# Second attention of a two-block transformer: value products with the values as stationary operand, two heads side by side, results already turned

## The chip, the cores and the metric

One Trainium2 chip, one of its cores. The metric is the device time of one execution in microseconds (us). TensorE is written PE in the profile, VectorE DVE, ScalarE ACT, GpSimd POOL, SyncE SP.

## The reference

Two transformer blocks on 512 tokens of width 1024, all in float32. The first has differential and stick-breaking attention and a convolved feed-forward network (FFN). The second has an FFN, a hybrid mixer and another FFN. The change lies in the mixer's attention and its output projection:

```python
q_a, kv_a, gate_a, q_b, kv_b = jnp.split(proj, offsets, axis=-1)
# heads of 64; 8 "NSA" query heads over 2 key/value heads, 8 "SWA" query heads over 2
o_cmp = jnp.einsum('bgrtc,bcgd->btgrd', p_cmp, vc)               # compressed keys, 31 of them
o_slc = selected_attention(q, ks, vs, sel_idx, slopes)           # top 16 of 8 blocks: all of them
o_win = banded_attention(q, kw, vw, slopes, NSA_WINDOW)          # window 512: the whole causal part
o_a = g[..., 0:1] * o_cmp + g[..., 1:2] * o_slc + g[..., 2:3] * o_win
o_b = banded_attention(q_b, k_b, v_b, slopes, SWA_WINDOW, sinks) # window 128, with a sink
o = jnp.concatenate([o_a, o_b], axis=-1)
return o @ w_out                                                 # 1024 x 1024
```

## The kernel before

All engines run programs written out by hand and joined by semaphores. Weights come from HBM in 1024-column units of 128 partitions through a ring of six slots (`stage`). ACT rounds each unit to `w_hi` (L619), POOL makes the remainder `w_lo` in two halves (L645), and each product is made of three matmuls, hi*hi, hi*lo, lo*hi.

The second attention (`at2`) is a list of 96 items. Items 0 to 63 (groups p = 0 to 3) are NSA heads: for each p and each block i of 128 queries, two branches times two heads g = 0, 1, each with b = i + 1 key blocks of 128. Items 64 to 95 (p = 4 to 7) are SWA heads, two for each i, with b = 1, 2, 2, 2. Items 2k and 2k+1 are always the two heads of a pair. There are 80 key blocks per head side in the NSA pairs together (32 pairs) and 28 in the SWA pairs (16 pairs).

Every engine runs the same loop of steps n, each engine its part of items n, n-1, n-2, ...:

- PE, even n: logits of items n and n+1 (L977): the heads' 64 channels stand on the upper and the lower 64 rows of the array. Every n: a few matmuls of filling, then the turns of item n-2's weights `W` by transposes (L1012), more filling, then the value product of item n-3 (L1019): stationary is the turned weight block (128x128), moving are 64 columns of values, in float32, so each matmul is two records in the trace.
- DVE: takes item n-4's result out of PSUM with the factor 1/sum times gate (L1081, L1078), then item n's logits plus bias with their row minimum (L1110), then for item n-1 reciprocal and gate factor (L1131, L1132, L1135).
- ACT: exp of item n-1 with its sum (L1056, L1057), copy of item n-2's turned weights to SBUF (L1064).

"Filling" is dense work that PE draws from a generator: 9 projection chunks of 24 matmuls and 96 matmuls of the compression's small network (L1262 to L1266), then, from step 84, the output projection: `pe_turn1` turns the finished outputs O (L1163), ACT and DVE split them into `T_hi` (L1187) and `T_lo` (L1200), and `pe_wo1` (L1210) multiplies. The table `FILL2` says how many at each step, with `(early, late)` for before and after the turns, and halves where it has one number:

```python
FILL2 = [4] * 48 + [6] * 4 + [0] + [6] * 4 + [0] + [3] * 8 + [0] + [3] * 8 + [0] + [3] * 8
FILL2 = FILL2 + [(0, 4), 0] + [(0, 4), (3, 0)] * 5 + [(3, 12), (12, 6), 6]
```

The compressed branch is hung on steps 49 to 77 by hooks: its own value product (L1612, four hooks at steps 70 to 76) and `dve_cmp_add` (L1620) add to O. Waits in the turns: `pe.wait_ge(a.exp_done, it.exps)`, that is, ACT's exp alone; DVE's factors come after. After step 99 `pe_wo_rest` makes the rest of the output projection (192 matmuls in all), and the last FFN follows (L548).

Of the kernel before, what the change touches and what calls it, by code (L numbers as in the profile page):

```python
# [39 lines left out]
P = 128  # L40
T = 512
# [65 lines left out]
SPARED = 4  # L107
WO_NEXT = {1: (1,), 3: (2,), 4: (3,), 5: (4,), 6: (5, 6)}
# [4 lines left out]
def unit_order():  # L113
# [11 lines left out]
    return order + [U_WO2 + j for j in WO_ORDER] + list(range(U_UP3, N_UNITS))  # L125
# [29 lines left out]
TURN_ORDER = [[c if kind == "diff" else 4 + c for kind, c in GROUPS1], [0, 1, 2, 3, 4, 6, 5, 7]]  # L155
# [3 lines left out]
FILL2 = FILL2 + [(0, 4), 0] + [(0, 4), (3, 0)] * 5 + [(3, 12), (12, 6), 6]  # L159
# [46 lines left out]
def build(nc, weights, x_t, params, rows, table_t, bias_line, out_t):  # L206
    with ExitStack() as top:
# [98 lines left out]

        def cmp_PT(h):
            return scratch[:, bass.ts(h, P)]
# [117 lines left out]
        n_ffn2 = Norm("ffn2", 7, "fold", X, order=WO_ORDER)  # L426
# [186 lines left out]

        def act_hi(act, u):

            if u < N_UNITS:
                slot = u % RING
                act.wait_ge(loaded[slot], 16 * (u // RING + 1))
                act.activation(w_hi[:, slot, :], stage[:, slot, :], ACT.Copy).then_inc(hi_done, 1)  # L619
# [201 lines left out]

        def item(items, **what):
            items.append(Item(**what))
# [24 lines left out]
        for p in range(8):  # L848
            c, q = p % 4, queries2(p)
            groups2.append(len(items2))  # L850
            for i in range(TB):
                if p < 4:
                    k0, nk, s0 = full(i)
                    for branch in range(2):
                        k = HOME2[("ks", "kw")[branch]]
                        for g in range(2):
# [5 lines left out]
                                 out=O[:, i, bass.ts(h, HD)], add=(branch == 1),  # L862
                                 gate=gates[:, i, 3 * h + 1 + branch:3 * h + 2 + branch], sink=None)
                else:
                    k0, nk = max(i - 1, 0) * P, min(i + 1, 2) * P
                    k = HOME2["kb"]
                    for g in range(2):
# [5 lines left out]
                             out=O[:, i, T + h * HD:T + (h + 1) * HD], add=False, gate=None,  # L873
                             sink=row[:, ROW_SINK + h:ROW_SINK + h + 1])
        for items in (items1, items2):
            pre, at = 0, 0
            for n, it in enumerate(items):
# [4 lines left out]
                it.dv = it.out.shape[-1]  # L882
# [71 lines left out]
        def item_bank(it):  # L954

            return ITEM_PS + it.n % 3

        def pe_attn(pe, a, fill=None, per_item=()):
# [31 lines left out]
            for n in range(len(items) + 3):  # L990
                f = per_item[n] if n < len(per_item) else 0
                early, late = f if isinstance(f, tuple) else (f - f // 2, f // 2)
# [10 lines left out]
                if 2 <= n < len(items) + 2:  # L1003
# [3 lines left out]
                    else:  # L1007
                        pe.wait_ge(a.comb if it.kind == "diff" else a.exp_done, it.exps)
                    if it.n >= 3:
# [5 lines left out]
                if n >= 3:  # L1015
# [9 lines left out]
        def act_attn(act, a, link, after):  # L1025
            items = a.items
            for n in range(len(items) + 2):
# [31 lines left out]
                if n >= 2:  # L1059
                    it = items[n - 2]  # L1060
                    act.wait_ge(a.turned, it.n + 1)
                    if it.n >= 2:
                        act.wait_ge(a.pv_done, it.n - 1)
                    act.activation(WT[:, it.n % 2, 0:it.nk], PS[:, item_bank(it), 0:it.nk],  # L1064
                                   ACT.Exp if it.kind == "sb" else ACT.Copy).then_inc(a.wt_ready, 1)
# [3 lines left out]
        def dve_attn(dve, a, link, after):  # L1069
            items = a.items  # L1070
            for n in range(len(items) + 4):
                if n >= 4:
# [3 lines left out]
                    if it.kind == "soft" and it.add:  # L1076
                        dve.wait_ge(a.o_done, it.n)
                        dve.scalar_tensor_tensor(out=it.out, in0=pv, scalar=it.st[:, 6:7], in1=it.out,  # L1078
                                                 op0=ALU.mult, op1=ALU.add).then_inc(a.o_done, 1)
                    elif it.kind != "sb":  # L1080
# [5 lines left out]
                if n < len(items):  # L1086
# [5 lines left out]
                    if n >= 4:  # L1092
# [21 lines left out]
                if 1 <= n < len(items) + 1 and items[n - 1].kind != "sb":  # L1114
# [14 lines left out]
                    else:  # L1129
# [13 lines left out]
        o_turned = [sem("o_turned1"), sem("o_turned2")]  # L1143
# [4 lines left out]
        def pe_turn1(pe, b, g):  # L1148
            k, bank = TURN_ORDER[b][g], 7
            if b == 0:  # L1150
                pe.wait_ge(o_ready, g + 1)
            elif g < 4:
                pe.wait_ge(cm["used"], TB)
            else:
                pe.wait_ge(at2.o_done, groups2[6] if g < 6 else len(items2))
            if b == 0 and 1 <= g <= SPARED:
# [1004 lines left out]
```

## Time and profile before

| | us |
|---|---|
| median of 3 runs | 1645.12 |
| lowest, highest | 1644.98, 1645.23 |
| profiled execution, span first to last instruction | 1643.2 |
| PE busy | 1623.6 (99%) |
| second attention, first logits to first FFN matmul | 1037.7 to 1271.5 |
| granted TensorE clock | 0.999 of full |

The profiled execution shows 1643.2 us as its span; the timed runs are about 1.9 us longer. Busy PE time includes a matmul's modelled end, so two records that overlap count once and a short pause between matmuls may show as busy.

### The profile page before, as it was taken

The numbers are of one execution on the slowest core, as the hardware profiler recorded it, in microseconds if no ns is written. First come the engines' busy times: TensorE is split into PE (matmuls) and PEld (weight loads), VectorE is DVE, ScalarE is ACT, GpSimd is POOL, SyncE is SP. The second block draws the span as 40 slices with busy tenths as digits, with TensorE's granted clock in tenths as the row PEclk, the third lists the DMA queues.
The fourth block names the chain that finished last, engine by engine and source line by source line (L and its number), as shares of the span: only waits on it lengthen the run. The fifth ranks groups of instructions, "written<-read, shape, count | busy, mean of one in ns | idle before, by whom it ended". The sixth has DMA issues, their size and how long they took to land.

```text
span 1643.2 us, 21043 instructions
## 1 busy us (share of the span) xinstructions
PE 1623.6 (99%) x8100; PEld 1349.0 (82%) x8100; DVE 701.2 (43%) x1404; ACT 674.6 (41%) x1183; POOL 759.2 (46%) x581
## 2 busy tenths in 40 slices
PE   9999999999999999999999999999999999999997
PEld 7787888888888888888888888888888888888886
DVE  7276747874444227322113225555773311112224
ACT  6356645543334325422223224567563422223322
POOL 7424454564445552744445552543114544444550
PEclk9999999999999999999999999999999999999999
DMA  5411102323222231323232322212002222223221
GB/s 205 148 52 52 52 1 103 129 90 103 92 101 95 97 101 61 116 96 102 90 103 90 103 92 101 91 66 78 27 27 96 97 94 99 99 94 103 90 103 51
DMA packets 42115, 147.35 MB, mean 90 GB/s; under 512 B 4768, under 2 KB 5152, under 8 KB 42016
## 3 DMA queue, kind: packets, MB, share of 16 engines
q1 hardware_dynamic: 40680, 143.39, 25.7%
q10 hardware_dynamic: 1336, 2.63, 0.5%
q8 instruction: 64, 1.05, 0.3%
q14 instruction: 35, 0.29, 0.1%
HBM read 142.84 MB, written 3.41 MB: 89 GB/s over the span
## 4 chain that ended last, share of the span: by engine, by line
PE 82%; DVE 2%; issue 1%; ACT 1%; POOL 1%; DMA 0%; DVEq 0%; ACTq 0%; POOLq 0%
PE PS L587 20%; PE PS L589 20%; PE PS L588 20%; PE PS L1210 5%; PE PS L548 4%; PE PS L1221 3%; PE PS L1019 2%; PE PS L556 2%; PE PS L977 2%; PE PS L1012 1%; POOL w_lo L645 0%; DVE L L1110 0%; DMA stage<-in_weights 0%; PE PS L609 0%; ACT sq L1057 0%
## 5 line engine op out<-in xcount | busy, mean ns | idle before, releaser
L645 POOL TENSOR_TENSOR w_lo<-stage,w_hi 128x512 fp32r<-128x512 f32 x522 | 707.9, 1380 | 819.2 <-ACT w_hi L619 818.3
L619 ACT ACTIVATE w_hi<-stage 128x1024 fp32r<-128x1024 f32 x262 | 274.8, 1056 | 519.9 <-DMA stage<-in_weights 516.0
L587 PE MATMUL PS<-H_hi,w_hi 128*128 128x512 f32 x992 | 386.1, 389 | 0.4 <-DVE rcol L1407 0.4
L588 PE MATMUL PS<-H_lo,w_hi 128*128 128x512 f32 x992 | 386.0, 389 | 0.0
L589 PE MATMUL PS<-H_hi,w_lo 128*128 128x512 f32 x992 | 385.9, 389 | 0.0
L587 PEld LDWEIGHTS PS<-H_hi,w_hi 128*128 128x128 f32 x992 | 186.2, 188 | 39.0 <-DVE rcol L1407 0.7
L589 PEld LDWEIGHTS PS<-H_hi,w_lo 128*128 128x128 f32 x992 | 186.2, 188 | 38.9
L588 PEld LDWEIGHTS PS<-H_lo,w_hi 128*128 128x128 f32 x992 | 186.2, 188 | 38.7
L587 PE MATMUL PS<-A_hi,w_hi 128*128 128x512 f32 x528 | 205.6, 389 | 0.3 <-DVE A_lo L756 0.3
L589 PE MATMUL PS<-A_hi,w_lo 128*128 128x512 f32 x528 | 205.4, 389 | 0.0
L588 PE MATMUL PS<-A_lo,w_hi 128*128 128x512 f32 x528 | 205.4, 389 | 0.0
L771 DVE TENSOR_TENSOR conv<-PS,rstd 128x512 f32<-128x512 f32 x88 | 56.5, 686 | 342.8 <-PE PS L589 333.7
L756 DVE TENSOR_TENSOR A_lo<-A,A_hi 128x512 fp32r<-128x512 f32 x66 | 84.0, 1278 | 227.2 <-ACT A_hi L700 227.2
L587 PEld LDWEIGHTS PS<-A_hi,w_hi 128*128 128x128 f32 x528 | 99.1, 188 | 21.7 <-DVE A_lo L756 1.2
L588 PEld LDWEIGHTS PS<-A_lo,w_hi 128*128 128x128 f32 x528 | 99.1, 188 | 20.7
L589 PEld LDWEIGHTS PS<-A_hi,w_lo 128*128 128x128 f32 x528 | 99.1, 188 | 20.4
L1019 PEld LDWEIGHTS PS<-V,tmp 128*128 128x128 f32 x672 | 93.8, 191 | 7.7
L1064 ACT ACTIVATE tmp<-PS 128x256 f32<-128x256 f32 (+3 forms) x144 | 59.4, 412 | 90.4 <-PE PS L1012 89.8
L1019 PE MATMUL PS<-V,tmp 128*128 128x64 f32 (+1 forms) x672 | 91.5, 264 | 0.0
L781 DVE SCALAR_TENSOR_TENSOR conv<-tmp,par,conv 128x511 f32<-128x511 f32 (+1 forms) x88 | 78.2, 944 | 4.3 <-ACT conv L723 4.2
L1221 PE MATMUL PS<-H_hi,w_hi 128*128 128x512 f32 x168 | 74.6, 444 | 0.9 <-DVE QB L940 0.9
L1221 PE MATMUL PS<-H_hi,w_lo 128*128 128x512 f32 x168 | 71.2, 424 | 0.0
(234 smaller groups left out, 2048.2 us busy)
## 6 DMA issues: line engine op xcount, KB each, us to landing
stage<-in_weights SPq DMA_DIRECT2D x262, 512.0 KB, 3.2
out_t<-Y SPq DMA_DIRECT2D x8, 256.0 KB, 2.0
X<-in_x_t SPq DMA_DIRECT2D x3, 512.0 KB, 8.8
bias_line<-bias_line ACTq DMA_DIRECT2D x1, 1270.0 KB
strip<-bias_line ACTq DMA_DIRECT2D x1, 1024.0 KB, 5.0
stage<-in_weights SPq DMA_DIRECT2D x2, 256.0 KB, 4.6
V<-QF SPq DMA_DIRECT2D x4, 128.0 KB, 2.3
V<-QF SPq DMA_DIRECT2D x4, 127.8 KB, 2.4
```

The lines of the kernel that those rows point to most:

```text
L548: pe.matmul(PS[:, j, :], w[:, (u0 + j) % RING, bass.ts(c, P)], H_hi[:, c, :], start=(k == 0 and w is w_hi), stop=False)
L587: pe.matmul(out, a, h_hi, start=first, stop=False, skip_group_check=skip)
L588: pe.matmul(out, a, h_lo, start=False, stop=False, skip_group_check=skip)
L589: return pe.matmul(out, b, h_hi, start=False, stop=last, skip_group_check=skip)
L619: act.activation(w_hi[:, slot, :], stage[:, slot, :], ACT.Copy).then_inc(hi_done, 1)
L645: lo = pool.tensor_tensor(w_lo[:, slot, cols], stage[:, slot, cols], w_hi[:, slot, cols].bitcast(F32), ALU.subtract)
L756: dve.tensor_tensor(A_lo[:, f % DEEP, :], A[:, f, :], A_hi[:, f % DEEP, :].bitcast(F32), ALU.subtract).then_inc(a_lo_done, 1)
L781: dve.scalar_tensor_tensor(out=y, in0=z[j][:, 0:T - back], scalar=c, in1=y, op0=ALU.mult, op1=ALU.add).then_inc(conv_step, 1)
L1019: mm = pe.matmul(PS[:, item_bank(it), 0:it.dv], WT[:, it.n % 2, bass.ts(kb, P)], it.v[kb], start=(kb == 0), stop=(kb == it.nk // P - 1))
L1064: act.activation(WT[:, it.n % 2, 0:it.nk], PS[:, item_bank(it), 0:it.nk], ACT.Exp if it.kind == "sb" else ACT.Copy).then_inc(a.wt_ready, 1)
L1210: mm = pe.matmul(PS[:, j, :], w[:, u % RING, cols], h, start=(g == 0 and x == 0), stop=(g == 7 and x == 2))
L1221: mm = pe.matmul(PS[:, bank, :], w[:, u % RING, bass.ts(k, P)], h[:, k, :], start=(k == 0 and x == 0), stop=(k == KC - 1 and x == 2))
```

## The change

The second attention's value product is turned round. Stationary are 64 columns of values (128 keys), moving the turned weights of 128 queries, and the result lands as 64 channels x 128 queries: head g = 0 on PSUM partitions 0 to 63 and g = 1 on 64 to 127 of bank 5, one call `soft_heads` for a pair, at odd steps, five steps behind its first item. Both branches of a pair accumulate in PSUM. So the 1/sum and gate factors can no longer be put on the result's rows; DVE puts them on the weights `W` (128 x 128b) before the turns, and the turns wait for that (`a.comb`). Outputs no longer need turning: for p < 4 DVE copies a finished 128x128 block to `O_flat`, where the compressed branch's product (also in turned form, 32 matmuls of 64 columns instead of 8) is added, and `act_sum_hi`/`dve_sum_lo` split the sum; for p >= 4 ACT and DVE split straight from PSUM. Weight rows of the output projection have another order, so its 8 units are loaded by four DMAs each. A step's filling stands in one piece behind the turns.

```diff
+WO_ORDER2 = [6, 7, 0, 1, 2, 3, 4, 5]
-    return order + [U_WO2 + j for j in WO_ORDER] + list(range(U_UP3, N_UNITS))
+    return order + [U_WO2 + j for j in WO_ORDER2] + list(range(U_UP3, N_UNITS))
-FILL2 = FILL2 + [(0, 4), 0] + [(0, 4), (3, 0)] * 5 + [(3, 12), (12, 6), 6]
+FILL2 = FILL2 + [0, 0] + [4, 3] * 5 + [1] + [6, 6, 6]
 # items
-out=O[:, i, bass.ts(h, HD)]
+out=PS[g * HD:(g + 1) * HD, HEADS_PS, bass.ts(i, P)]      # HEADS_PS = 5
 # PE
+            def soft_heads(n):
+                it = items[n]
+                if not it.add and n > 0:
+                    pe.wait_ge(a.o_done, 4 * it.group + it.i)
+                pe.wait_ge(a.wt_ready, n + 2)
+                blocks = it.nk // P
+                for kb in range(blocks):
+                    for x in (it, items[n + 1]):
+                        mm = pe.matmul(x.out, x.v[kb], turned_weights(x)[:, bass.ts(kb, P)],
+                                       start=(kb == 0 and not x.add),
+                                       stop=(kb == blocks - 1 and (x.add or x.gate is None)))
+                mm.then_inc(a.pv_done, 1)
-                early, late = f if isinstance(f, tuple) else (f - f // 2, f // 2)
+                early, late = f if isinstance(f, tuple) else (0, f) if a is at2 else (f - f // 2, f // 2)
-                        pe.wait_ge(a.comb if it.kind == "diff" else a.exp_done, it.exps)
+                        pe.wait_ge(a.comb, it.exps)
+                if a is at2:
+                    if n >= 5 and n % 2 == 1:
+                        soft_heads(n - 5)
 # DVE, item n-1
-                        if it.gate is not None:
-                            c = link(dve.tensor_scalar(it.st[:, 6:7], it.st[:, 6:7], it.gate, None, ALU.mult))
-                            after(c)
-                        dve.sem_inc(a.comb, 1)
+                        w = W[:, it.n % 2, 0:it.nk]
+                        if it.gate is None:
+                            dve.tensor_scalar(w, w, it.st[:, 6:7], None, ALU.mult).then_inc(a.comb, 1)
+                        else:
+                            dve.tensor_scalar(w, w, it.st[:, 6:7], it.gate, ALU.mult, ALU.mult).then_inc(a.comb, 1)
 # the splits that replace pe_turn1, act_turn1 and dve_turn1 of the second attention
+        def act_heads_hi(p, i, pair):
+                act.wait_ge(at2.pv_done, pair + 1)
+                act.activation(T_hi[:, p, bass.ts(i, P)], PS[:, HEADS_PS, bass.ts(i, P)], ACT.Copy).then_inc(heads_hi, 1)
+        def dve_heads_lo(p, i):
+                dve.tensor_tensor(T_lo[:, p, cols], PS[:, HEADS_PS, cols], T_hi[:, p, cols].bitcast(F32), ALU.subtract)
 # compressed branch
-                    mm = pe.matmul(PS[:, 7, bass.ts(h % 2, 256)], cmp_PT(h), vc4[:, bass.ts(h // 4, 256)], start=True, stop=True)
+                for i in range(TB):
+                    for g in range(2):
+                        mm = pe.matmul(PS[g * HD:(g + 1) * HD, 7, bass.ts(i, P)], vc4[:, bass.ts(4 * g + i, HD)],
+                                       cmp_PT(4 * g + pair), start=True, stop=True)
 # hooks
+            hook(at2, "act", at + 29 + pair, act_sum_hi(pair))      # steps 78 to 81
+            hook(at2, "dve", at + 30 + pair, dve_sum_lo(pair))      # steps 79 to 82
+        for p in range(8):
+            for i in range(TB):
+                last = groups2[p] + (4 * i + 2 if p < 4 else 2 * i)
+                if p < 4:
+                    hook(at2, "dve", last + 6, dve_heads_out(p, i, last // 2))
+                else:
+                    hook(at2, "act0", last + 6, act_heads_hi(p, i, last // 2))
+                    hook(at2, "dve", last + 6, dve_heads_lo(p, i))
 # loads of the output projection
+                for g in range(2):
+                    for l in range(2):
+                        sp.dma_start(there[bass.ts(g, HD), :, :, l, :],
+                                     here[bass.ts(l, HD), :, g, :, :]).then_inc(loaded[u % RING], 16)
```

## Rows read from the trace of the kernel before

**Rows 1.** Windows: NSA steps, SWA steps, rest of the projection; busy us (x records) of PE, PEld, DVE, ACT, POOL.

```profile
1037.70:1170.70 133.00, 131.91 (x1009) 113.57 (x1008) 78.17 (x341) 86.39 (x226) 48.60 (x36) 1.00 0.21 69
1170.70:1228.40 57.70, 55.59 (x415) 47.01 (x414) 44.24 (x184) 39.24 (x139) 7.56 (x6) 1.00 0.09 29
1228.40:1271.50 43.10, 43.10 (x201) 35.59 (x201) 13.57 (x25) 14.33 (x21) 16.89 (x13) 1.00 0.24 86
```

**Rows 2.** Timeline of PE (start, us, what): a value product, then logits.

```profile
1102.76 1.00 PE L1019 MATMUL PS<-V,tmp 128*128 128x64 f32 x8
1103.69 0.49 PE L977 MATMUL PS<-K_f,QF 64*128 64x128 f32 x4
```

**Rows 3.** Timeline of PE: logits and turns; column-tiled products; the small network's filling.

```profile
1224.19 0.71 PE L977 MATMUL PS<-B_f,QB 64*128 64x128 f32 x8
1224.84 0.44 PE L1012 MATMUL PS<-ident,sq 128*128 128x128 f32 x2
...
1141.05 0.43 PE L1019 MATMUL PS<-V,tmp 128*128 128x64 f32 x2
1141.41 0.43 PE L1481 MATMUL PS<-hid,par 128*64 128x31 f32 x8
1141.77 1.39 PE L1486 MATMUL PS<-par,hid 128*31 128x64 f32 x32
...
1087.55 0.31 PE L1262 MATMUL PS<-w_hi,kp_hi 128*62 128x256 f32 x1
1087.70 0.28 PE L1264 MATMUL PS<-w_lo,kp_hi 128*62 128x256 f32 x1
```

**Rows 4.** Chain that ended last (start, us, what): a turn of O, projection matmuls.

```profile
1243.54 0.44 PE PS L1163 x4
1243.98 4.09 PE PS L1210 x18
```

**Rows 5.** Groups of DVE by shape (busy, mean ns): logits read, reciprocal, a tile scaled.

```profile
L1110 DVE CUSTOM_DVE_ANT_0 L<-PS,strip 128x512 f32<-128x512 f32 x24 | 16.3, 691 | 5.8 <-PE PS L977 3.6 <-DVE O L1081 0.9 <-DVE O L1078 0.7
L1132 DVE RECIPROCAL stat<-stat 128x1 f32<-128x1 f32 x96 | 15.4, 160 | 8.4 <-ACT sq L1057 7.0
L564 DVE TENSOR_SCALAR conv<-X,par 128x512 f32<-128x512 f32 x2 | 1.0, 480 | 0.0
```

**Rows 6.** Timeline, DVE then POOL: a scaling of SBUF tiles while POOL works.

```profile
1024.46 4.98 DVE L2057 TENSOR_SCALAR V<-tmp 128x256 f32<-128x256 f32 x4
...
1022.83 8.99 POOL L645 TENSOR_TENSOR w_lo<-stage,w_hi 128x512 fp32r<-128x512 f32 x7
```

**Rows 7.** Timeline of a late SWA step, DVE and ACT.

```profile
1226.46 0.48 DVE L1110 CUSTOM_DVE_ANT_0 L<-PS,V,row 128x256 f32<-128x256 f32 x1 [0.17 <-ACT sq L1057]
...
1226.87 0.21 DVE L1131 TENSOR_SCALAR stat<-stat 128x1 f32<-128x1 f32 x1
...
1227.06 0.29 ACT L1056 ACTIVATE stat<-row,stat 128x1 f32<-128x1 f32 x1
...
1227.12 0.16 DVE L1132 RECIPROCAL stat<-stat 128x1 f32<-128x1 f32 x1
1227.25 0.49 ACT L1057 ACTIVATE sq<-L,stat 128x256 f32<-128x256 f32 x1
...
1227.65 0.19 ACT L1057 ACTIVATION_READ_ACCUMULATOR sq<-L,stat 128x1 f32 x1
```

**Rows 8.** DMA issues (KB each, us to landing); then the SP queue's own timeline.

```profile
stage<-in_weights SPq DMA_DIRECT2D x262, 512.0 KB, 3.2
V<-QF SPq DMA_DIRECT2D x4, 128.0 KB, 2.3
...
1049.79 0.60 SPq L1696 DMA_DIRECT2D V<-QF  x1
```

**Rows 9.** Timeline of POOL and waits of the weight loads around the end of the projection.

```profile
1257.14 15.59 POOL L645 TENSOR_TENSOR w_lo<-stage,w_hi 128x512 fp32r<-128x512 f32 x11 [8.96 <-ACT w_hi L619]
...
PEld PS L548 <- POOL w_lo L645: 0.3, 1, 0.3
```

More of the change, by code:

```diff
@@ L152 @@
 NAT_BANK = [4, 5, 7, 2]
-TURN_ORDER = [[c if kind == "diff" else 4 + c for kind, c in GROUPS1], [0, 1, 2, 3, 4, 6, 5, 7]]
+TURN_ORDER = [[c if kind == "diff" else 4 + c for kind, c in GROUPS1], list(range(8))]
 FILL2 = [4] * 48 + [6] * 4 + [0] + [6] * 4 + [0] + [3] * 8 + [0] + [3] * 8 + [0] + [3] * 8
-FILL2 = FILL2 + [(0, 4), 0] + [(0, 4), (3, 0)] * 5 + [(3, 12), (12, 6), 6]
+FILL2 = FILL2 + [0, 0] + [4, 3] * 5 + [1] + [6, 6, 6]
 def fill2_steps(name):
@@ L612, in pe_token_unit, with loads_of @@
             m.then_inc(unit_done, 1)
+        def loads_of(u):
+            return u // RING + 1 + 3 * sum(1 for v in range(U_WO2, min(u + 1, U_UP3)) if v % RING == u % RING)
         def act_hi(act, u):
@@ L861, in build @@
                                  v=[V[:, 0, kb, branch * P + g * HD:branch * P + (g + 1) * HD] for kb in range(nk // P)],
-                                 out=O[:, i, bass.ts(h, HD)], add=(branch == 1),
+                                 out=PS[g * HD:(g + 1) * HD, HEADS_PS, bass.ts(i, P)], add=(branch == 1),
                                  gate=gates[:, i, 3 * h + 1 + branch:3 * h + 2 + branch], sink=None)
@@ L881, in build @@
                 it.bank = [(it.map0 + m) % 3 for m in range(len(it.maps))]
-                it.dv = it.out.shape[-1]
+                it.dv = HD if it.kind == "soft" else it.out.shape[-1]
                 it.st = stat[:, n % 4, :]
@@ L988, in ahead @@
                 return n < len(items) and n % 2 == 0 and items[n].kind == "sb" and items[n].i in (1, 2)
-            for n in range(len(items) + 3):
+            def soft_heads(n):
[10 more added lines that the diff above has]
+                mm.then_inc(a.pv_done, 1)
+            for n in range(len(items) + (4 if a is at2 else 3)):
                 f = per_item[n] if n < len(per_item) else 0
-                early, late = f if isinstance(f, tuple) else (f - f // 2, f // 2)
+                early, late = f if isinstance(f, tuple) else (0, f) if a is at2 else (f - f // 2, f // 2)
                 for what in a.hooks["pe0"].get(n, []):
@@ L1026, in act_attn @@
             items = a.items
-            for n in range(len(items) + 2):
+            for n in range(len(items) + (6 if a is at2 else 2)):
                 for what in a.hooks["act0"].get(n, []):
@@ L1070, in dve_attn @@
             items = a.items
-            for n in range(len(items) + 4):
-                if n >= 4:
+            for n in range(len(items) + (6 if a is at2 else 4)):
+                if n >= 4 and a is at1:
                     it = items[n - 4]
@@ L1075, in dve_attn @@
                     pv = PS[:, item_bank(it), 0:it.dv]
[L1076 to L1080, printed above, removed]
+                    if it.kind == "diff":
                         dve.tensor_scalar(it.out, pv, it.st[:, 6:7], None, ALU.mult).then_inc(a.o_done, 1)
@@ L1164, in pe_turn1 @@
                 if i == TB - 1:
[L1165 removed]
+                    mm.then_inc(o_turned, 1)
                 yield
@@ L1173, in wait_turned, with act_turn1 @@
         def wait_turned(eng, b, g):
[L1175 removed]
+            if b == 1 and g < 4:
+                eng.wait_ge(o_split[1], g + 1)
+            elif b == 1:
+                eng.wait_ge(at2.o_done, 4 * g + 4)
+            elif g < SPARED:
                 eng.wait_ge(o_pool, g + 1)
             else:
[L1178 to L1182 removed]
+                eng.wait_ge(o_split[0], g + 1 - SPARED)
+        def act_turn1(act, g):
+            act.wait_ge(o_turned, g + 1)
+            if g < SPARED:
                 if g >= 2:
@@ L1300, in pe_wo_rest @@
                 if at == EARLY:
-                    pe.wait_ge(a.o_done, len(a.items))
+                    pe.wait_ge(a.o_done, len(a.items) if b == 0 else 32)
+                    pe.wait_ge(a.wt_ready, len(a.items))
                 run(pe_wo1(pe, b, at, range(8)))
```

176 lines of the change are left out of this document (107 added, 69 removed).

## The prediction

> **What bounds the kernel now.** I read the page's busy shares first, then windows over the second attention, then the chain of waits and the timeline inside it. The page (the table above) has PE busy 99% of the span. The windows say where that is real: in the 133.0 us of NSA steps PE is busy 131.9, while DVE works 78.2, ACT 86.4 and POOL 48.6; in the 57.7 us of SWA steps PE is busy 55.6 and DVE 44.2; in the last 43.1 us PE alone counts, and the clock is full throughout [rows 1]. So what leaves PE is gained, as long as no new wait takes its place. Slack of DVE is large in the first window and small in the second.
>
> **PE work of the value product.** Before, 8 records start at 1102.76 and the logits behind them at 1103.69; less the change of form in between that is 0.111 us a record [rows 2]. A record streams only 64 columns, so the 128-column weight load sets that pace. A pair of items with b key blocks each has 4b records: 0.444b us. Afterwards a record loads 64 columns and streams 128. The nearest rows of two products side by side in the array are the logits: 8 records of 128 columns from 1224.19 to the turns at 1224.84, 0.65 us, where one after the other would take 8 x 0.107 = 0.86 [rows 3]; 0.43 of the 0.65 is four pairs at 0.107, 0.22 leaving the form and the first load. For halves of the columns the row is L1481: 8 records in 0.36 us from 1141.41 to 1141.77, 0.045 each, and L1486 with 32 records in 1.39 [rows 3], below what one load after the other of the full array shows. I take side by side: 2b x 0.107 = 0.214b a pair. The other bound is one after the other, 0.428b, no gain at all.
>
> Each pair also has one change of form more (full array, columns, rows, full). L1019's two records to L1481 take 0.36 us where 0.22 is their pace, so 0.14 a change; with the exposed first load I take 0.25 a pair, between 0.14 and 0.36 (in and out both new) [rows 3]. Gain a pair: 0.23b - 0.25. Over 32 NSA pairs (80 blocks) 18.4 - 8.0 = 10.4 us; over 16 SWA pairs (28 blocks) 6.4 - 4.0 = 2.4 us.
>
> The Trainium skill, TensorEngine Tiling (Array Packing), Key Properties, says that a change of tiling mode drains the engine while tiles inside one mode work in parallel. By this rule, the trace agrees on both: the 0.14 and the 0.65.
>
> **Other PE work.** The 32 turns of O go: 0.44 us for 4 [rows 4], 3.5 us; 8 of them stood in the pure PE stretch. The compressed product goes from 16 records at 0.216 (256 columns at the 0.107 pace of 128) to 64 half-width ones, 32 pairs at 0.107, the same 3.4 us, plus four times in and out, 0.28: +1.1 us. Sum of PE work: -10.4 - 2.4 - 3.5 + 1.1 = **-15.2 us**.
>
> **New wait 1, turns behind DVE.** Before, item n-1's turns needed ACT's exp, done long before. Now DVE must first scale W, and in an even step N it comes to item N-1 only after reading item N's logits. From the logits' end: 0.04 to start, 0.61 of L1110's 0.69 (512 wide) until the next starts, 0.20 for the reciprocal, then the scaling, 0.06 to PE. Scaling a 128x512 tile in SBUF with a factor from SBUF took 480 ns [rows 5]; with two factors I take 0.54, and 0.34 at 128 wide. Chain: 0.85, 1.04, 1.25, 1.45 us for b = 1 to 4. PE's cover is item N-2's turns (0.109b) and the filling, now all behind them: 4 x 0.229 [rows 4] gives 1.07, 1.18, 1.28, 1.39. That just holds; this is what the filling in one piece is worth. But at steps 18 to 29 and 36 to 47 the filling is the small network's, 0.14 each [rows 3], and the cover 0.71 to 1.03: short by 0.14 to 0.42, 0.29 on average over 12 pairs, 3.5 us. With 3 instead of 4 at steps 58 to 63: 0.8. Sum **+4.3 us** (from 2 to 7).
>
> **New wait 2, DVE behind POOL.** Four scalings of 128x256 took 4.98 us under POOL's row of L645, 1.25 each, POOL's own pace (8.99 for 7), while double that width took 0.48 with POOL still [rows 5, 6]. So a scaling that meets a POOL operation waits for its end. POOL is busy 37% of the NSA window [rows 1]; of 32 scalings of odd items (the even ones have a whole step) 12 meet it, and wait half of 1.3 us less the little slack, 0.42: **+5.0 us**. Bounds: 0, if the in-place form does not behave so, and 12 x 0.65 = 8. The small factors (L1132) never wait; what is new is that a whole tile is scaled.
>
> The Trainium skill, SBUF — State Buffer, section SBUF: two separate sides, says that GpSimd and a VectorE operation that uses both port pairs lock each other out for a whole instruction. By this rule, the trace agrees: 1.25 against 0.48.
>
> **New wait 3, the SWA ring.** `act_heads_hi` stands ahead of ACT's exp of item N-1 and waits for the value product at the end of PE's step N-1. From that result (0): copy and start 0.22; L1056, L1057 and its read 0.79; DVE's L1131 and L1132 0.45, scaling 0.35, PE at 1.95 [rows 7]; its turns 0.22, filling 3 x 0.229, change 0.13, product with its latency 0.66: 3.65 us a pair, where PE's own work is 3.22 (logits 0.75, turns 0.43, filling 1.37, product 0.65). Steps 70 to 76 have the compressed product as cover. So 0.4 at the pairs of 78, 80, 82; 0.2 at five pairs with 4 and 3 fillings; 1.0 at 84 without filling; 1.0 at 96 with one; and the sums' splits on ACT and DVE at 78 to 82 exceed the period by 1.4. **+5.6 us** (3 to 9). The old waits of these last steps on the T_hi, T_lo handover go: -1.5.
>
> **Loads.** 8 units by four DMAs each: SP needs 0.60 an issue, and 128 KB took 2.3 us to land [rows 8], so a unit lands some 4.6 to 5 us after its release, not 3.2. Six of them have many us of lead. The seventh is released late; behind it POOL works without a pause to the FFN, whose first load waited 0.3 us for it [rows 9]. So the delay shows: **+1.5 us** (0 to 4). SP's other loads queue behind; they follow with more lead.
>
> **Sum.** -15.2 + 4.3 + 5.0 + 5.6 - 1.5 + 1.5 = -0.3 us: span 1642.9, and with the 1.9 between span and runs a time of **1644.8 us**. PE loses 15 us of work and gives nearly all back as waits.
>
> **Rivals.** *The waits hide (faster).* If POOL does not hold the scaling, or its hits fall where the fillings cover, the 5.0 go; if also the chain is 0.2 shorter than I add it up, some 2.5 of the 4.3: 1637.3. For it: my cover and chain differ by a tenth of a us. Against: rows 6. *DVE is late (slower).* At steps 55 to 82 the compressed branch's operations of 0.7 us and the new sums' splits stand on DVE, some 14 us, with DVE already busy 44 of 57.7 us [rows 1]. Before, DVE was two steps ahead of anyone; now every second step PE waits for its scaling. DVE needs about 3.0 us a pair of the 3.7; over 14 pairs 10 us are free, and 4 to 6 stand over, with the uneven placing 6: 1651. It decides once DVE's work between two logits passes the pair's period. *No two products side by side.* Then +0.214 x 108 = 23 and 3.4 in the compressed branch: 1671. Rows 3 speak against it; float32 streams of 128 different columns into both halves they don't show.
>
> **Chances.** Forecast 0.37, waits hide 0.34, DVE late 0.23, not side by side 0.06. Range 1634.5 to 1654: from both waits gone and the rest of the 4.3 too, to DVE late at its upper end; the serial case stays outside. The forecast's own range is 1641.5 to 1648. What a measurement of this kernel can tell from no change is 0.2%, 3.3 us: faster 0.34, the same 0.37, slower 0.29.
>
> **What the profile after would show.** The value product's records half-width, in pairs a few ns apart, 0.107 between pairs (else the third rival); no L1163 in the second attention; PE idle at L1012 put down to DVE W, not ACT, some 10 us in the NSA window, more at the small network's steps; single scalings of up to 1.4 us under POOL; in the SWA steps a period of 3.6 us and ACT waiting for the value product; the FFN's first load waiting 1 to 2 us for w_lo. The prediction is wrong if the NSA window (133.0 us before) shrinks by over 4 us, or if the SWA window grows by over 6.

## The result, and the profile after

The changed kernel takes 1657.0 us (median of 4 runs, 1656.0 to 1658.5), the kernel before 1645.1: a ratio of 1.0073, with an interval of 1.0061 to 1.0086. The change makes it 12 us slower. I had forecast 1644.8 us, with 1634.5 to 1654 as the range.

In the changed kernel the logits are L993, the turns of W L1045, the value product L1015, the projection L1286 and L1297; DVE reads logits at L1148 and scales W at L1176 (NSA, with gate) and L1174 (SWA). The windows of the profile after, NSA steps and then everything up to the last FFN, columns as in [rows 1]:

```profile
1037.20:1178.90 141.70, 126.66 (x1001) 92.83 (x1000) 89.61 (x299) 86.65 (x228) 49.48 (x36) 0.99 0.21 64
1178.90:1282.60 103.70, 95.27 (x641) 68.65 (x639) 60.59 (x215) 55.07 (x170) 24.56 (x19) 1.00 0.17 52
```

The NSA steps take 141.7 us in place of 133.0, and PE, busy for nearly all of them before [rows 1], is now idle for 15. The rest takes 103.7 in place of 100.8. So 8.7 of the 11.6 us by which the two profiled executions differ here lie in the NSA steps, where I had forecast a gain of 1.1.

The waits of PE in the profile after (us in total, times, longest us):

```profile
PE PS L1045 <- DVE sq L1176: 14.7, 18, 3.7
PE PS L1045 <- DVE sq L1174: 6.3, 9, 1.9
PE PS L1286 <- POOL w_lo L659: 1.7, 1, 1.7
```

Before, the turns named no wait for DVE, and in the NSA steps only two for ACT's exp:

```profile
PE PS L1012 <- ACT sq L1057: 1.0, 2, 0.5
```

Now 27 of the 96 items' turns wait for the scaling of W (named `sq`, its memory), 21.0 us in all. By the timeline 24 of them, 15.3 us, stand at odd steps: there the scaling comes behind DVE's reading of the logits that PE wrote one step before. Three, 5.6 us, stand at even steps (2, 34 and 52), where the scaling has a whole step of room: at step 2 it stands behind DVE's work on the gates, at 34 and 52 ACT's exp itself was late. The longest wait, at step 34, on the timeline of all engines (start, us):

```profile
1104.29 2.34 POOL L1523 TENSOR_TENSOR scratch<-V,par 128x992 f32<-128x992 f32 x1
...
1106.66 1.03 ACT L1529 ACTIVATE kp_hi<-scratch 128x992 fp32r<-128x992 f32 x1 [3.32 <-POOL scratch L1523]
1107.60 0.39 ACT L1093 ACTIVATE sq<-L,stat 128x128 f32<-128x128 f32 x1
1107.77 2.27 POOL L1535 TENSOR_TENSOR kp_lo<-scratch,kp_hi 128x992 fp32r<-128x992 f32 x1 [1.14 <-ACT kp_hi L1529]
...
1108.11 0.16 DVE L1170 RECIPROCAL stat<-stat 128x1 f32<-128x1 f32 x1 [4.45 <-ACT sq L1093]
1108.31 1.82 DVE L1176 TENSOR_SCALAR sq<-sq,stat,gates 128x128 f32<-128x128 f32 x1
...
1110.19 0.33 PE L1045 MATMUL PS<-ident,sq 128*128 128x128 f32 x1 [3.73 <-DVE sq L1176]
...
1113.38 1.69 PE L1015 MATMUL PS<-O,V 128*64 128x128 f32 x16
```

Read it from the top. POOL forms the windows of the compression; ACT stands 3.3 us in its queue waiting to copy them, with the exp that PE needs behind the copy. The scaling starts at 1108.31 and meets POOL's next operation: 1.82 us for a tile that takes 0.35 when POOL is still. PE waits 3.73 us. Then comes a second loss, in windows of PE's busy time and granted clock:

```profile
1110.00:1112.00 2.00, 1.81 (x8) 1.45 (x9) 1.57 (x9) 0.87 (x5) 0.05 (x1) 0.81 0.03 8
1112.00:1114.00 2.00, 2.00 (x10) 1.25 (x10) 0.51 (x1) 0.44 (x3) 0.00 (x0) 0.50 0.00 0
1114.00:1116.00 2.00, 2.00 (x25) 1.71 (x22) 0.44 (x2) 0.00 (x0) 0.00 (x0) 0.84 0.72 240
```

From 1111.2 to 1114.6, after the idle time, the granted clock stood at 0.50, the 1.2 GHz level; then it was at 1.00 again. The same 16 records of the value product took 1.62 us to the next logits (1113.38 to 1115.00) where one pair earlier they had taken 1.02; the fillings came 0.43 us apart, not 0.23. That is some 1.6 us more.

A named wait is also less than what PE loses. PE's timeline at a short one:

```profile
1085.49 0.28 PE L1352 MATMUL PS<-w_hi,kp_lo 128*62 128x256 f32 x1
1085.61 0.28 PE L1348 MATMUL PS<-w_hi,kp_hi 128*62 128x256 f32 x1
1086.27 0.44 PE L1045 MATMUL PS<-ident,sq 128*128 128x128 f32 x2 [0.39 <-DVE sq L1176]
```

Matmuls start 0.12 apart and each lasts 0.28, one over the other. From 1085.61 to 1086.27 are 0.66 us: 0.54 lost, 0.39 named. The first turn behind a wait then takes 0.057 more than others. So each wait costs some 0.2 us beside its name, 5 us for the 27.

### The profile page after: what moved, and what is told of

The parts are those of the page before. It is cut to its first block, busy times and chain, and to the rows that moved or that the text cites. A ratio compares the mean times of both kernels' runs of the same rounds, so it can differ in the third digit from the quotient of the medians.

```text
span 1654.2 us, 20890 instructions
## 1 busy us (share of the span) xinstructions
PE 1615.3 (98%) x8116; PEld 1314.9 (79%) x8116; DVE 716.0 (43%) x1368; ACT 676.3 (41%) x1195; POOL 760.4 (46%) x581
## 4 chain that ended last, share of the span: by engine, by line
PE 79%; DVE 3%; ACT 2%; POOL 2%; issue 1%; DMA 1%; SPq 0%; DVEq 0%; ACTq 0%; POOLq 0%
PE PS L597 20%; PE PS L598 20%; PE PS L599 20%; PE PS L1286 4%; PE PS L558 4%; PE PS L1297 2%; PE PS L566 2%; PE PS L993 2%; PE PS L1045 2%; POOL w_lo L659 1%; PE PS L1015 1%; DVE sq L1176 1%; DVE L L1148 1%; DMA stage<-in_weights 1%; ACT w_hi L633 0%
## 5 line engine op out<-in xcount | busy, mean ns | idle before, releaser
L598 PE MATMUL PS<-H_lo,w_hi 128*128 128x512 f32 x992 | 386.0, 389 | 0.0
L1045 PE MATMUL PS<-ident,sq 128*128 128x128 f32 x336 | 65.5, 288 | 21.6 <-DVE sq L1176 14.7
L1045 PEld LDWEIGHTS PS<-ident,sq 128*128 128x128 f32 x336 | 38.8, 141 | 47.9 <-DVE sq L1176 23.9
L1297 PE MATMUL PS<-H_hi,w_hi 128*128 128x512 f32 x168 | 73.0, 434 | 0.0
L1297 PE MATMUL PS<-H_hi,w_lo 128*128 128x512 f32 x168 | 69.2, 412 | 0.0
L1297 PE MATMUL PS<-H_lo,w_hi 128*128 128x512 f32 x168 | 68.7, 409 | 0.0
```

The lines of the kernel that those rows point to most:

```text
L598: pe.matmul(out, a, h_lo, start=False, stop=False, skip_group_check=skip)
L1045: mm = pe.transpose(PS[:, item_bank(it), bass.ts(kb, P)], W[:, it.n % 2, bass.ts(kb, P)], ident[:, :])
L1297: mm = pe.matmul(PS[:, bank, :], w[:, u % RING, bass.ts(k, P)], h[:, k, :], start=(k == 0 and x == 0), stop=(k == KC - 1 and x == 2))
```

## The experiments

All times are medians; each ratio is to the kernel before in the same session, with its interval. Unless it says otherwise an edit is made to the changed kernel (1657.0). The times of one kernel spread by up to 4 us (the four edits from 1641.6 to 1645.2), so a difference of some 1.5 us between two rows is shown only where all single times of one lie below those of the other.

| run | us | ratio |
|---|---|---|
| no scaling | 1630.4 | 0.9912 [0.9898, 0.9925] |
| no scaling, one head and then the other | 1635.8 | 0.9943 [0.9931, 0.9956] |
| scaling with three operands | 1660.9 | 1.0098 [1.0084, 1.0112] |
| w_lo in four | 1659.3 | 1.0088 [1.0074, 1.0101] |
| exp to PSUM | 1662.2 | 1.0103 [1.0090, 1.0117] |
| window earlier | 1654.3 | 1.0058 [1.0045, 1.0070] |
| copy of the heads behind exp | 1654.0 | 1.0058 [1.0044, 1.0071] |
| w_hi between | 1654.0 | 1.0053 [1.0039, 1.0066] |
| scaling first | 1652.8 | 1.0051 [1.0039, 1.0064] |
| one load | 1655.5 | 1.0063 [1.0049, 1.0077] |
| filling split | 1651.7 | 1.0043 [1.0030, 1.0055] |
| filling ahead | 1650.9 | 1.0035 [1.0022, 1.0047] |
| three edits | 1644.5 | 0.9999 [0.9991, 1.0008] |
| four edits | 1643.0 | 0.9988 [0.9979, 0.9996] |
| four edits, exp to PSUM | 1645.5 | 1.0004 [0.9995, 1.0013] |
| four edits, filling ahead | 1643.8 | 0.9998 [0.9989, 1.0007] |
| four edits, filling split | 1642.7 | 0.9985 [0.9976, 0.9994] |

**Is it the waiting or PE's work?** Scaling left out (the weights stay unscaled and ungated):

```diff
-                        pe.wait_ge(a.comb, it.exps)
+                        pe.wait_ge(a.comb if it.kind == "diff" else a.exp_done, it.exps)
-                            dve.tensor_scalar(w, w, it.st[:, 6:7], it.gate, ALU.mult, ALU.mult).then_inc(a.comb, 1)   # and the branch without gate
+                        dve.sem_inc(a.comb, 1)
```

> The changed kernel without the scaling of W by DVE; the turns wait for ACT's exp, as before the change (the weights stay unscaled and ungated). Theory A, the loss is waiting behind the scaling: PE's idle time put down to it is 14.7 us at L1176 and 6.3 us at L1174, 27 times; each wait also loses about 0.2 us of the overlap of one matmul with the next (665 ns from one start to the next at 1085.61, 118 ns is the pace, 0.39 us are named), 5 us; and the 1.7 us of low clock behind the longest. Some comes back as waits for exp. Time 1631 to 1640 us, no idle put down to W's scaling. Theory B, the value product's PE work is what is dearer than I counted, and the waits only stand where PE would be late anyway: no more than 8 us come back, 1649 or more.

1630.4 us, 26.6 less than the changed kernel and 14.5 less than before the change. The windows of this run:

```profile
1037.55:1160.57 123.02, 120.75 (x999) 92.81 (x999) 55.06 (x236) 84.88 (x227) 48.69 (x36) 1.00 0.24 74
1160.57:1256.88 96.31, 93.26 (x641) 69.34 (x639) 49.60 (x182) 54.77 (x171) 24.50 (x19) 1.00 0.18 56
```

What is left of PE's waits at the turns, now for exp (the longest at step 34 again):

```profile
PE PS L1045 <- ACT sq L1093: 2.2, 3, 1.5
```

Theory A, and a little more than I gave it. The NSA steps are 10.0 us shorter than before the change, the rest 4.5: what the change takes from PE's work is really there. In both this run and the changed kernel two records of a pair start 7 ns apart and the pairs 0.109 us, as forecast.

In this kernel, the two heads' blocks one after the other:

```diff
-                for kb in range(blocks):
-                    for x in (it, items[n + 1]):
+                for x in (it, items[n + 1]):
+                    for kb in range(blocks):
```

> The kernel without any scaling (1630.4 us, PE nearly without waits), and in it the value product's key blocks of one head first and then those of the other, in place of one of each in turn. Only PE's work changes. If a product in one half of the columns runs beside one in the other only when they follow each other in pairs, each of the 108 pairs (80 in NSA, 28 in SWA steps) costs one pace more: at 0.107 us 11.6 us in all, 1642. If a half-width product has half the pace anyway (L1481's and L1486's 0.045), 1630 to 1632, and the gain of the change comes from the width and not from two heads in one bank.

1635.8, 5.4 more, between the two answers: about half of the 11.6. On PE's timeline the records of one head now start 0.109 us apart, but where the second head's begin, some still start beside the first's. The order in pairs is worth 5.4 us here.

**How much of it does POOL hold?** In the changed kernel, of the 96 scalings the 70 that overlapped with no POOL operation took the same time for each size (345 to 348 ns at 128 columns with gate, 545 to 548 at 512); the 26 that met one took up to 1818 ns, 11.0 us more in all. How much of PE's waiting stands directly behind such a scaling can be read there: 10 of the 27 waits, 11.4 us, and of these the part by which the scaling in front was held is 6.5 us at most. The other 17 waits, 9.6 us, stand behind scalings that met nothing. (A hold further back in DVE's queue can make a later scaling late; this count leaves that out.) Three attempts to get rid of the hold:

```diff
-                            dve.tensor_scalar(w, w, it.st[:, 6:7], it.gate, ALU.mult, ALU.mult)
+                        dve.scalar_tensor_tensor(out=w, in0=w, scalar=it.st[:, 6:7], in1=by, op0=ALU.mult, op1=...)
```

> The changed kernel with the scaling written as an operation with three operands (W times 1/sum times a broadcast gate; without gate the third is passed over). Theory A, POOL's operations hold the two-operand form: the scalings of 1.2 to 1.8 us (1078.60, 1089.33, 1108.31, 1130.26, 1223.73) become 0.3 to 0.6, PE's waits of 1.1, 1.4, part of 3.7, 1.3 and 1.9 behind them go, and some 0.2 to 0.4 at ten lesser ones; if the new form is not held, 7 to 11 us less: 1646 to 1650. Theory B, the form is held as well, or its own duration (a 512-wide one may take 0.7 in place of 0.55) is paid at every second step: within 2 us of the changed kernel, or slower by up to 3.

1660.9, 3.9 us slower, a little beyond theory B's 3: PE's waits for the scaling rose from 21.0 to 24.6 us. 28 of these scalings met POOL and took 11.5 us more in all, and a free one is longer (751 ns at 512). The Trainium skill, GPSIMD Engine Reference, Specifications, names contention "with DVE instructions in a 2-port perf mode or with two SBUF inputs"; the form with three operands, all in SBUF, is of the second kind. By this rule, the trace agrees: 28 meetings, 11.5 us. Whether the form with two operands ran in such a mode no row shows. The second attempt:

```diff
-            for half in range(2):
-                cols = bass.ts(half, T)
+            for part in range(4):
+                cols = bass.ts(part, T // 2)
```

> The changed kernel with POOL's w_lo in four operations of 256 columns in place of two of 512 (in the whole kernel). Theory A, a scaling that meets POOL waits for the end of its operation: the longest holds shrink from 1.3 to 0.65 us, the waits of 1.1, 1.4, 1.3 and 1.9 us at PE by half or so; 2 to 4 us less, 1653 to 1655, the scalings of over 1.2 us at L1176 and L1174 gone. Theory B, DVE comes in between two POOL operations only by chance, or POOL's four starts cost what is gained: within 1 us of the changed kernel.

1659.3, 2.3 us slower: nearer to theory B, though outside its 1 us. The hold fell only to 9.5 us, and a quarter took POOL 0.79 us where a half took 1.38, so POOL was busy 846 us and not 760. PE's waits for scaling and w_lo sum to 22.4 us, no more than in the changed kernel (22.7), but the granted clock was at 0.50 for 10.2 us of this profiled execution (from 1044.5, 1112.8 and 1273.2), in place of 3.4. So the 2.3 us more go with the clock rather than with longer waits; what ties the clock to the edit is open. The third attempt lets DVE read PSUM:

```diff
-  act.activation(W[:, it.n % 2, 0:it.nk], LM(0, it.n)[:, 0:it.nk], ACT.Exp, ...)
+  act.activation(PS[:, it.bank[0], 0:it.nk], LM(0, it.n)[:, 0:it.nk], ACT.Exp, ...)
-  dve.tensor_scalar(w, w, ...)
+  dve.tensor_scalar(w, PS[:, it.bank[0], 0:it.nk], ...)
+  pe.wait_ge(a.comb, items[n - 2].exps)     # ahead of the logits
-  act.wait_ge(a.turned, it.n - 1)           # exp no longer writes W
+  dve.wait_ge(a.turned, it.n - 1)           # the scaling does
```

> The changed kernel with ACT's exp written into the item's own PSUM bank of logits (read already) and DVE's scaling from there into W; PE's logits of a pair wait until the scaling of the item that last used the bank is done. In the changed kernel every scaling that met no POOL operation took 0.29 to 0.55 us and spread by 5 ns a size, and the 26 that met one took 11.0 us more in all; none of the 96 readings of logits from PSUM was longer for POOL. Theory A, POOL holds only operations that leave PSUM out: the 11.0 us go, single scalings take 0.3 to 0.7 us without exception, and the waits of 1.1, 1.4, 1.3 and 1.9 us at PE with them; less what the wider scaling (0.69 in place of 0.55 at 512) and the logits' new wait cost, 3 to 7 us less, 1650 to 1654. Theory B, POOL holds it all the same, or the new wait of the logits costs as much: 1656 or more.

DVE's groups by shape, the first row of the changed kernel, the second of this one (busy us, mean ns):

```profile
L1176 DVE TENSOR_SCALAR sq<-sq,stat,gates 128x384 f32<-128x384 f32 x16 | 11.4, 711 | 0.6
```

```profile
L1178 DVE TENSOR_SCALAR sq<-PS,stat,gates 128x384 f32<-128x384 f32 x16 | 10.8, 677 | 0.6
```

And PE's waits in this run (us in total, times, longest), L995 the logits and L1047 the turns:

```profile
PE PS L995 <- DVE sq L1178: 8.9, 10, 2.7
PE PS L1047 <- DVE sq L1178: 7.7, 19, 0.8
```

The mechanism of theory A is shown: 24 scalings met POOL and were as long as the others of their size to within 5 ns. The time is theory B's, 1662.2. With the SWA steps (L1176) the turns wait 12.6 us in place of 21.0, but each scaling is longer (809 ns for 512) and the logits now wait 10.8 us, so the waits for the scaling are 2.4 us more. Between the two profiled executions are 7.3 us. Part of the rest goes with the clock: it was at 0.50 for 13.6 us in place of 3.4, half of it here (columns as in the windows above):

```profile
1227.14:1233.96 6.82, 6.07 (x29) 4.43 (x27) 3.44 (x14) 3.44 (x11) 2.50 (x2) 0.50 0.06 17
```

So the hold is real, 11.0 us of DVE's time, but this run doesn't price its part of PE's loss; a version that frees the scaling and makes nothing else wait was not found.

**What makes the scaling late?** POOL's second window forming one step earlier, ahead of its w_lo:

```diff
-            hook(at2, "pool", at, pool_windows(s))
+            hook(at2, "pool", at - s, pool_windows(s))
```

> The changed kernel with POOL's second forming of the compression's windows one step earlier, ahead of the w_lo of its step, so that ACT's copy of it has no wait in front of its exp. Theory A, the ring POOL, ACT, DVE, PE at step 34 alone costs the 3.7 us of PE idle and 1.7 us at a lower clock behind it: 4 to 5.5 us less, 1651.5 to 1653, and the granted clock stays at 1.00 there. Theory B, the exp is late for another reason (ACT's own work): no more than 1.5 us less.

1654.3, 2.7 us less, between the two theories. The 3.7 us at step 34 went with the low clock behind it (granted 1.00 from 1100 to 1118), but the earlier POOL operation met another scaling, and that made a wait of 1.6 us at step 31. The hold was moved, not removed. The low clock came back elsewhere too: from 1222.6 to 1226.0 it stood at 0.50, behind the wait of 1.8 us at step 87, which the changed kernel has as well (1.9) without a drop. ACT's copy of the heads goes behind the exp:

```diff
-                    hook(at2, "act0", last + 6, act_heads_hi(p, i, last // 2))
+                    hook(at2, "act", last + 6, act_heads_hi(p, i, last // 2))
```

> The changed kernel with ACT's copy of a finished value product into T_hi behind its exp and its copy of the turned weights, not ahead of them. My prediction's wait 3 took 0.4 us a pair for the copy's place. Theory A: the pairs of the SWA steps 78 to 94 take 3.3 in place of 3.5 us, 2 to 4 us less in all, 1653 to 1655. Theory B, in these steps the wait is DVE's queue (and POOL at 1223), and the product is only later: within 1 us of the changed kernel, or slower, since the next product waits for the same bank.

1654.0, 2.9 us less, theory A: the waits at L1174 fell from 6.3 to 3.9 us. ACT's w_hi goes between exp and copy:

```diff
-            hook(at2, "act", at + 1, lambda act, u=U_FILL2 + e: act_next(act, u))
+            hook(at2, "act_mid", at + 1, lambda act, u=U_FILL2 + e: act_next(act, u))   # between exp and copy
```

> The changed kernel with ACT's w_hi (1.05 us, one a unit of the filling, 17 in the second attention) between the exp of its step and the copy of the turned weights, a copy that waits for PE's turns anyway, not behind that copy and so ahead of the next exp. Theory A, w_hi makes that exp, its scaling and PE's turns late by up to 1 us, and POOL's w_lo, which starts as w_hi ends, then meets that very scaling; with w_hi in the gap both end: 4 to 8 us less, 1649 to 1653. Theory B, the exp has a step's slack for it and only the chance meeting with POOL counts, which just falls elsewhere: within 1.5 us of the changed kernel.

1654.0, 3.0 us less: below theory A's 4 to 8, above B's. POOL met 30 scalings and not fewer (11.7 us of hold), so these meetings fell elsewhere, as B says; PE's waits at the turns fell from 21.0 to 19.3 us. The last of these edits swaps DVE's two parts in even steps:

```diff
+                for part in (weigh, read) if a is at2 and n % 2 == 0 else (read, weigh):
+                    part()
```

> The changed kernel with one thing in another order: in the even steps DVE scales the weights of the item before first and reads the logits that PE has just written second (before: the other way round). Theory A, PE waits because this scaling stands in DVE's queue behind a reading that itself waits for PE's logits: the chain of 0.85 to 1.45 us leaves the step, most of the 21 us of idle at the turns goes, except where ACT's exp is late itself (the 3.7 us at step 34); 8 to 14 us less, 1643 to 1649. Theory B, DVE and POOL's hold on it are the limit, whatever the order, and the reading comes later instead: at most 2 us less.

1652.8, 4.2 us less, half of the least that theory A said. In its profiled execution (1654.9 us) the waits at odd steps fell from 15.3 to 10.2 us, but those at even steps rose from 5.6 to 8.4. At step 34 PE still waited 3.9 us, since exp itself was late there.

**Together:**

> The changed kernel with three edits together: the scaling ahead of the reading in the even steps, POOL's second window forming one step earlier, ACT's copies into T_hi behind its exp. Alone the second gave 2.7 us and the third 2.9. Theory A, the places are apart and the gains add: 1657 - 2.7 - 2.9 and 8 to 14 for the first, 1637 to 1643, faster than the kernel before the change (1645), and within 8 to 13 us of the kernel without any scaling (1630.4). Theory B, DVE or POOL is the limit: 1648 or more.

1644.5: 12.5 us less than the changed kernel, where the three alone sum to 9.8. Why the sum is more than its parts no run takes apart; one edit may uncover what another one hid.

> The three edits of the run before and w_hi between exp and copy. Left in the run with three are 12.8 us of idle at the turns and 14 us to the kernel without scaling. Theory A, most of the waits left stand behind w_hi or its w_lo: 4 to 8 us less than 1644.5, 1636 to 1640, faster than before the change. Theory B, what is left is POOL's hold wherever w_lo falls: 1643 or more.

1643.0, 1.5 us less than with three, where w_hi alone gave 3.0; but the single times of the two kernels overlap (1641.6 to 1645.2 and 1643.8 to 1646.0), so this step is not shown. The time is theory B's. Against the kernel before the change it is faster by 0.1%, with the interval just below 1. Left are 12.2 us of waits at the turns, and 25 scalings that meet POOL take 15.8 us more. With exp to PSUM on top:

> The four edits (1643.0 us; there 25 scalings met POOL and took 15.8 us more) with exp in PSUM too. Theory A, POOL's hold is what is left of the waits: 12.2 us of idle at the turns fall to 5 or less, 1634 to 1639, some 0.5% faster than before the change. Theory B, the chain itself and the logits' new wait are: 1642 or more.

1645.5, theory B. The turns' waits fell from 12.2 to 1.7 us, as theory A wanted, but the logits now wait 13.3 us (22 times), and the clock was at 0.50 for 10.2 us in the profiled execution, where the four edits had none.

**The loads.** One DMA a unit in place of four (the rows of the second WO are then not those of the heads):

> The changed kernel with one DMA for each unit of the second WO in place of four (the rows of these units are then not those of the pairs of heads). My prediction took 1.5 us for the four. Theory A: PE's wait for w_lo in the projection falls from 1.7 to 0.3 us or less and the time by 1 to 1.5 us, 1655.5 to 1656. Theory B: ACT and POOL have work in between that hides the later landing, and the wait comes from the projection's shorter lead, not from the DMAs: within 0.5 us of the changed kernel.

1655.5, 1.5 us less, and the 1.7 us wait of L1286 for w_lo is gone: theory A. All its single times (1654.5 to 1655.7) lie below those of the changed kernel.

**The cover.** The filling again in two halves (below), and then all of it ahead of the turns (`(f, 0)` for the second attention):

```diff
-                early, late = f if isinstance(f, tuple) else (0, f) if a is at2 else (f - f // 2, f // 2)
+                early, late = f if isinstance(f, tuple) else (f - f // 2, f // 2)
```

> The changed kernel with each step's filling in two parts again, one ahead of the turns and one behind. My prediction had the filling in one piece behind the turns as the cover of DVE's chain. In the odd steps the part ahead (2 x 0.23 us) covers the turns' wait for the scaling directly, in the even ones too. Theory A, the waits move to other places and the sum stays: within 3 us of the changed kernel, and the waits at the turns fall while none comes elsewhere of the same size. Theory B, the block behind is needed for the turned weights' copy and the product (each waits 0.5 us and more): 3 us slower or worse.

> The changed kernel with each step's filling in one block ahead of the turns. In two parts it gave 5.3 us. From an even step's logits to the turns that wait for the chain behind them PE has 4 fillings and the turns of the item before if the block stands behind the turns, 6 if it is split, 8 if it stands ahead (0.23 us each). Theory A, this cover is what counts: as much again as the split or somewhat less, since the wait of 3.5 us at step 34 stays, 1647 to 1651. Theory B, the turned weights come so late that the product or the next turns (two banks) wait, or that ACT's next exp does: 1652 or more.

1651.7 and 1650.9: 5.3 and 6.0 us less than with the block behind the turns. The waits of the run with halves:

```profile
PE PS L1045 <- DVE sq L1176: 11.8, 13, 3.5
PE PS L1045 <- DVE sq L1174: 3.7, 5, 1.3
```

It is the odd steps that gain: their waits sum to 15.3 us with the block behind the turns, 9.9 with halves, 6.3 with the block ahead, while those at even steps stay (5.6, 5.7, 6.1). Between halves and ahead the times (0.7 us) are too close to tell apart.

On the four edits it does no more:

> The four edits (1643.0 us) with the filling ahead of the turns. Theory A, the waits for the chain and for POOL's hold are both covered: idle at the turns from 12.2 to 4 us or less, 1634 to 1639. Theory B, the edits had already covered what the filling could: 1641 or more.

> The four edits (1643.0 us) with the filling in two parts, ahead of the turns and behind them. Theory A, half of what the filling ahead gives: 1638 to 1641. Theory B, no more cover is wanted: 1642 to 1644.

1643.8 and 1642.7 against 1643.0, no difference outside the spread, theory B for both. With the filling ahead, the waits at the turns fell to 7.3 us, but the value product now waited 3.4 us for the result's copy (`T_lo` and `O`).

## Why the prediction was wrong

**PE's work: right.** I took -15.2 us, and with 1.5 back for the loads and 1.5 of old waits gone that is 15.2 us less than before; without scaling the kernel is 14.5 us faster. By windows: product -10.4 forecast, -10.0 measured over the NSA steps; the rest -4.8 by my terms (-2.4 - 3.5 + 1.1 - 1.5 + 1.5), -4.5 measured. These windows hold waits as well as work, so they show the sum and not each term. The third rival (no two products side by side) fell.

**The waits: 14.9 us forecast, 26 measured.** Each window of the changed kernel less that of the kernel without scaling: 141.7 - 123.0 = 18.7 in the NSA steps, where waits 1 and 2 were to be 9.3, and 103.7 - 96.3 = 7.4 in the rest, where wait 3 was to be 5.6. That is 11.2 of the 12.2 us by which I was off. What failed are three things that the sum put at nothing:

- *The chain's start.* I let it begin with PE's logits, with ACT always in time, and left the even items out: "the even ones have a whole step". ACT's queue also has the compression's copy, 17 w_hi of 1.05 us and the heads' copies ahead of some exp. Before, turns needed that exp alone, and the trace before has two waits for it, of 0.5 us each, in all the NSA steps. Now reciprocal and scaling stand behind it. The three waits at even steps are 5.6 us, 3.73 of them at step 34; without scaling 1.5 us is left there.
- *What a wait costs.* I counted idle time alone. There were 0.2 us more for each of the 27, 5 us.
- *The clock.* There were 1.6 us of low clock behind the longest wait. That is in the profiled execution, of 1656.0 us with a mean granted clock of 0.998; the other three have 0.995 to 0.996 and took 1656.7 to 1658.5 us, so they had more of it.

Together that is some 12 us; the kernel without scaling has 2.2 us of waits for exp too.

What I did price came out near its size. At odd NSA steps PE waited 9.0 us by name, 15 times, where waits 1 and 2 were to be 9.3. In like terms, of the scalings of odd NSA items 14 met POOL and were held 5.0 us; I had 12 and 5.0. Even NSA items had 9 more meetings (4.5 us) and the SWA items 3 (1.5 us). Part of this agreement is luck, for I had them meet by chance: in fact POOL's w_lo starts 0.08 us after w_hi ends, and ACT's next exp follows soon, for 14 of the 18 w_hi from 1042 to 1222 us with nothing in between. After each of the 18 the scaling that needed this exp met POOL.

One choice was wrong too, and I had called it a merit. *Wait 1* says "PE's cover is item N-2's turns (0.109b) and the filling, now all behind them", and "this is what the filling in one piece is worth". I started at the logits' end and looked only at the filling between them and the waiting turn of the next step: 4 behind the even step's turns. Halves keep 4 there (2 + 2) and put 2 more ahead of the odd step's turns, so 6. The block behind the turns was the worst of three places, by 5.3 and 6.0 us.

Some figures of the prediction don't come out of its own terms. The cover, 4 x 0.229 + 0.109b, is 1.03 to 1.35 us and not 1.07 to 1.39, and even 1.39 is less than the chain of 1.45, so "That just holds" was not so at four blocks. The range's lower end, with all of waits 1 and 2 gone, is 1635.5 and not 1634.5. A change of form is 0.04 us where the pace of 0.111 a record is worked out and 0.14 further on; with 0.14 the pace would have been 0.099 and the gain smaller. From their first record to what follows all 96 value products of the trace before take 47.1 us, 0.109 a record.

Wait 3 had its place right (the copy behind exp gave 2.9 us back), the loads their size (1.5 forecast, 1.5 measured), though PE waited for w_lo inside the projection and not at the FFN. The rival "DVE is late" put 6 us into the SWA steps; the loss was mainly in the NSA steps, where DVE was busy 90 of 142 us: its queue was not full, its work came late. My signs of being wrong, an NSA window shorter by 4 us or an SWA window longer by 6, did not include what came: an NSA window longer by 8.7. How PE's 26 us divide between POOL's hold and the order of the queues stays open, for no run removed the one and left the other as it was; the trace says only that the hold stands directly in front of at most 6.5 of the 21.0 us named.

## What to carry to other kernels

When a new dependency goes onto the critical engine, follow it back through every queue that it passes, and list what each of these queues puts in front at any step, hooks included; slack that no profile needed before is now the price. Cover for a wait is only what the critical engine has between the source and the waiting instruction, so put movable work ahead of the waiting instruction (here worth 6.0 us, and nothing beyond the spread on top of the four edits). And run once with the new work left out: it says at once whether the planned gain exists (here 14.5 us) and how much is waiting (26.6).

## What the runs showed of the hardware

- DVE's scaling of a tile in SBUF took longer in 24 of its 26 meetings with POOL (up to 1.8 us for 0.35), 11.0 us in all; the form with three operands 11.5 us in 28 meetings. The same scaling read from PSUM never did (24 meetings, all within 5 ns), but it is longer by itself, 0.81 for 0.55 us at 512 columns.
- Four POOL operations of 256 columns took 15% more in sum than two of 512 (0.79 against 1.38 us each).
- The granted clock fell to 0.50 some 1 us after PE had resumed from 3.7 us without work, and was back at 1.00 3.4 us later. The length of one wait does not say whether it falls: in the changed kernel a wait of 1.9 us left it at 1.00, in the run with the window earlier it fell behind one of 1.8, and in the four edits with exp to PSUM it stood at 0.50 from 1214.0 to 1220.8, with no wait of PE over 1.2 us there.
- Half-width products of two heads ran partly side by side even when not issued in pairs: 5.4 us were lost where full serial work would have cost 11.6.
